# Output projection as seven half-size products in chunks, its input rows formed on GpSimd alone

## The reference

```python
h = rms_norm(x, in_norm_g)
q, k, v, g, xr, gr, m_ret, m_rnn = split(h @ w_in)
y_ret = (silu(g) * head_norm(retention(rot(q), rot(k), v))) @ w_ret_o
y_rnn = (rg_lru(conv(xr)) * gelu(gr)) @ w_rnn_o
mixed = sigmoid(m_ret) * y_ret + sigmoid(m_rnn) * y_rnn
x = x + mixed @ w_out                      # the output projection: 1024 x 1024 by 1024 x 1024
h = rms_norm(x, ffn_norm_g)
up = causal_depthwise_conv(h @ w_up)
x = x + (silu(gate) * val) @ w_down        # gate, val = the halves of up
out = rms_norm(x, final_norm_g)
```

## Time and profile before

| | |
|---|---|
| median of 3 runs | 1991.19 us (1989.85 to 1991.75) |
| span of the profiled execution | 1988.8 us |
| TensorE, VectorE, ScalarE, GpSimd busy | 99%, 71%, 47%, 17% of the span |
| `reto` | 28 chunks, 672 matmuls of 128x512 |
| output projection | 768 matmuls of 128x256, 1248.4 to 1345.7 us |

### The profile page before, as it was taken

The page is one execution under the profiler, slowest core; times in us unless marked ns, Lnnn a source line. Parts: engine busy times, 40 slices in busy tenths (PEclk is TensorE's granted clock), DMA queues, the critical chain, the costliest instruction groups (busy, mean ns, idle before and its releaser), DMA issues.

```text
span 1988.8 us, 24558 instructions
## 1 busy us (share of the span) xinstructions
PE 1961.3 (99%) x9208; PEld 1639.4 (82%) x9208; DVE 1418.8 (71%) x1621; ACT 934.4 (47%) x1182; POOL 333.9 (17%) x277
## 2 busy tenths in 40 slices
PE   8999999999999999999999999999999999999998
PEld 6888888888888888888888787997888888888887
DVE  7877876776755445667777658658987888776766
ACT  6443353343445555555555443346544544543335
POOL 2000010010392000067775003100000000000000
PEclk9999999999999999999999999999999999999999
DMA  6343554445697443465668555532222222256523
GB/s 259 117 169 137 180 181 157 169 158 179 206 327 281 159 159 127 148 200 173 206 190 256 199 196 194 184 112 84 85 91 78 84 84 84 74 191 234 199 96 132
DMA packets 222205, 325.07 MB, mean 163 GB/s; under 512 B 11824, under 2 KB 150448, under 8 KB 221872
## 3 DMA queue, kind: packets, MB, share of 16 engines
q1 hardware_dynamic: 196800, 232.84, 35.5%
q0 software_dynamic: 22608, 85.99, 11.0%
q10 hardware_dynamic: 2720, 5.24, 0.8%
HBM read 223.36 MB, written 100.66 MB: 163 GB/s over the span
## 4 chain that ended last, share of the span: by engine, by line
PE 83%; DVE 9%; ACT 3%; DMA 2%; issue 2%; POOL 1%; ACTq 0%; SPq 0%; DVEq 0%; POOLq 0%
PE ps L346 27%; PE ps L348 27%; PE ps L347 27%; DVE ws L329 1%; DMA stg<-scr_y 1%; DMA raw<-scr_q 1%; PE ps L1219 1%; POOL qkvs L949 1%; POOL state_s L955 1%; DVE ysr L2415 0%; DVE wx L2155 0%; POOL ws L968 0%; DVE wsr L2408 0%; ACT ri L1648 0%; DVE th L2337 0%
## 5 line engine op out<-in xcount | busy, mean ns | idle before, releaser
L1501 ACT ACTIVATE wx<-raw 128x1024 fp32r<-128x1024 f32 (+1 forms) x152 | 137.3, 905 | 252.3 <-DVE raw L2131 131.4
L346 PE MATMUL ps<-xs,wx 128*128 128x512 f32 x612 | 239.1, 391 | 2.1 <-DVE xs L2578 1.6
L348 PE MATMUL ps<-xs,wx 128*128 128x512 f32 x612 | 238.3, 389 | 0.0
L347 PE MATMUL ps<-xs,wx 128*128 128x512 f32 x612 | 238.2, 389 | 0.0
L2155 DVE TENSOR_TENSOR wx<-raw,wx 128x1024 fp32r<-128x1024 f32 (+1 forms) x152 | 158.9, 1047 | 30.4 <-ACT wx L1501 30.2
L346 PE MATMUL ps<-sc,wx 128*128 128x512 f32 x448 | 174.4, 389 | 0.0
L348 PE MATMUL ps<-sc,wx 128*128 128x512 f32 x448 | 174.3, 389 | 0.0
L347 PE MATMUL ps<-sc,wx 128*128 128x512 f32 x448 | 174.3, 389 | 0.0
L1536 ACT ACTIVATE ub<-ps 128x512 f32<-128x512 f32 x112 | 66.9, 597 | 159.1 <-PE ps L348 156.4
L346 PEld LDWEIGHTS ps<-xs,wx 128*128 128x128 f32 x612 | 114.9, 188 | 28.4 <-issue 2.7
L348 PEld LDWEIGHTS ps<-xs,wx 128*128 128x128 f32 x612 | 114.9, 188 | 24.1
(11 more groups left out here) (289 smaller groups left out, 4849.2 us busy)
## 6 DMA issues: line engine op xcount, KB each, us to landing
raw<-w_in SPq DMA_DIRECT2D x80, 512.0 KB, 5.5
scr<-ost POOLq DMA_DIRECT2D x32, 1024.0 KB, 5.2
raw<-w_up SPq DMA_DIRECT2D x44, 512.0 KB, 4.2
tq<-w_down SPq DMA_DIRECT2D x88, 128.0 KB, 2.7
scr_t<-tq POOLq DMA_DIRECT2D x22, 512.0 KB, 3.2
scr_h<-vt POOLq DMA_DIRECT2D x11, 1024.0 KB, 4.3
tr<-w_ret_o SPq DMA_DIRECT2D x64, 128.0 KB, 3.9
scr_q<-tr POOLq DMA_DIRECT2D x16, 512.0 KB, 5.2
```

Source lines behind the costliest of these rows:

```text
L346: pe.matmul(out, w(HI), x(HI), start=first, stop=False, skip_group_check=True)
L347: pe.matmul(out, w(HI), x(LO), start=False, stop=False, skip_group_check=True)
L348: return pe.matmul(out, w(LO), x(HI), start=False, stop=last, skip_group_check=True)
L1501: act.activation(dst, src, ACT.Copy).then_inc(sem["f_hi"], 1)
```

## The change

The output projection becomes seven products of 512x512 blocks (`O_W`), in 14 chunks, two per product, run as `reto`'s are: chunk numbers go on from 28, with the same buffers `wsr` and `ysr`. 24 matmuls of 128x512 per chunk, 336 in all.

- Four combined weight blocks (t1 to t4) are made on GpSimd during `reto`: eight pieces, `out_pieces` loads (SyncE, behind `reto_w` of chunks 6, 8, 10 and 12), `out_combine` computes and stores to `scr_o`.
- `mixed(n)` is on GpSimd alone, product and addition, into `mixm` (float32, four blocks); GpSimd also makes the four combined activation blocks, two additions of 128x1024 each (`mixed_sum`). Its order: 12 pieces, two sums, 4 pieces, six sums.
- ScalarE and VectorE split weights and activations chunk by chunk (`outp_w_hi`, `outp_y_hi`, `outp_w_lo`, `outp_y_lo`).
- VectorE adds partial products to `x1` (`out_add`, `out_add_row`); the order of the products (`O_W`, `O_BANK`) lets banks 4 to 7 accumulate b11, then t2, then t3, with reads between.
- The transposes of the first half of the tokens stand behind chunk 38 and inside chunk 39; the norms of the rows 4 to 7 stand behind the last additions.

The lines on which the rest turns:

```diff
+O_W = ["t4", "t1", "b11", "t2", "t3", "b22", "b21"]
+O_BANK = [4, 0, 4, 4, 4, 0, 4]
+O_FIRST = [True, True, True, False, False, False, True]
+O_LAST = [True, False, False, False, True, True, True]
...
             for i in range(4, R_CHUNKS):
                 reto_w(i)
+                if i >= 6 and i % 2 == 0 and (i - 6) // 2 < O_PIECES // 2:
+                    out_pieces(i - 6)
+                    out_pieces(i - 5)
...
+                if i in (24, 25, 26, 27):
+                    mix_more(i - 21)
+            for v in range(4):
+                sp_.wait_ge(sem[f"tr_out{v}"], 16 * (R_PIECES + O_PIECES) // 4)
+            out_w(R_CHUNKS)
             sp_.wait_ge(*late_count("ry_lo", R_CHUNKS - 4))
             sp_.dma_start(x1[:, 0:4, :], x_t[:, 0:4, :]).then_inc(sem["x_re"], 16)
...
+            out_w(R_CHUNKS + 1)
+            mix_more(7)
...
+            def out_combine(j):
...
+                pool.tensor_tensor(tr[:, v, 0:2, :], tr[:, v, 0:2, :], tr[:, v, 1:3, :], ALU.subtract).then_inc(late_sem("tr_st"), 1)
+                pool.wait_ge(*late_count("tr_st", done + 1))
+                pool.tensor_tensor(tr[:, v, 2, :], tr[:, v, 0, :], tr[:, v, 2, :], ALU.add).then_inc(late_sem("tr_st"), 1)
+                pool.wait_ge(*late_count("tr_st", done + 2))
+                pool.tensor_tensor(tr[:, v, 3, :], tr[:, v, 3, :], tr[:, v, 2, :], ALU.subtract).then_inc(late_sem("tr_st"), 1)
...
+            def mixed(n):
                 half, t = mix_at(n)
                 pool.wait_ge(sem[f"mx_in{n // 2 % 3}"], 32 * (n // 6 + 1))
                 pool.wait_ge(sem["acc"], mix_acc(n))
                 pool.tensor_tensor(msg[:, n % 6, :], msg[:, n % 6, :], yacc[:, t, half * HALF:(half + 1) * HALF],
                                    ALU.mult).then_inc(sem["mx_mul"], 1)
+                pool.wait_ge(sem["mx_mul"], n + 1)
+                pool.tensor_tensor(mixm[:, 2 * half + t // 4, t % 4, :], msg[:, n % 6, :], mrb[:, n % 6, :], ALU.add
+                                   ).then_inc(sem["mx_f"], 1)
...
+            for i in range(R_CHUNKS, R_CHUNKS + 11):
+                outp(i)
+            pe.wait_ge(sem["xn_done"], 8)
+            pe.wait_ge(sem["x1_done"], 12)
+            for k in range(4):
+                turn2(k, 0, 4 + k)
+            outp(R_CHUNKS + 11, (0, 1))
...
-            pe.wait_ge(sem["x1_done"], 16)
+            pe.wait_ge(sem["x1_done"], 18)
             for k, bank in ((0, 4), (1, 5), (2, 2), (3, 3), (4, 6), (5, 7)):
                 turn2(k, 1, bank)
...
+            def outp_w_lo(i):
+                u = i % 2
+                dve.wait_ge(*late_count("rw_hi", i + 1))
+                dve.tensor_tensor(wsr[u][:, LO, :, :], raw[:, 1, 2 * u * HALF:2 * (u + 1) * HALF].rearrange("p (k c) -> p k c", k=2),
+                                  wsr[u][:, HI, :, :].bitcast(F32), ALU.subtract).then_inc(late_sem("rw_lo"), 1)
...
+            for i in range(R_CHUNKS + 2, R_CHUNKS + 11):
+                outp_w_lo(i)
+                outp_y_lo(i)
+                p, c, _ = outp_at(i)
+                if c == 0 and p < 5:
+                    for t in (0, 2):
+                        out_add(p - 1, t, 2)
...
+            out_add(6, 2, 1)
             s_lo(A12, a12f, 0, 3)
             s_lo(A12, a12f, 1, 4)
-            out_add(6, 1)
-            prep_lo(0, 0, "b1")
+            out_add(6, 3, 1)
+            norm2(4)
+            norm2(5)
             combine_t4(0, 0)
             prep_lo(0, 0, "t4")
             prep_lo(0, 0, "t2")
...
+            norm2(6)
+            norm2(7)
```

More of the change, by code:

```diff
@@ L1277, in turn2 @@
                 last.then_inc(sem["tr_ps"], 1)
[L1279 to L1284, removed]
-                    pe.wait_ge(sem["acc"], 6)
[L1286 to L1303, removed]
-                if m == 5:
-                    for k in range(4, 8):
-                        pe.wait_ge(*late_count("a11_in", k - 3))
-                        turn2(k, 0, k)
@@ new lines, in outp_free, with outp @@
+            def outp_free(p, t):
+                if p == 0:
+                    pe.wait_ge(sem["acc"], 6)
+                elif p == 1:
+                    pe.wait_ge(sem["acc"], 7 + t)
+                elif p < 6:
+                    pe.wait_ge(sem["x1_done"], {2: 1, 3: 5, 4: 7, 5: 3}[p] + t // 2)
+                else:
+                    pe.wait_ge(sem["x1_done"], 12)
+                    pe.wait_ge(*late_count("a12_in", 4))
+            def outp(i, tiles=range(4)):
+                p, c, _ = outp_at(i)
+                u = i % 2
+                pe.wait_ge(*late_count("rw_lo", i + 1))
+                pe.wait_ge(*late_count("ry_lo", i + 1))
+                for t in tiles:
+                    if c == 0:
+                        outp_free(p, t)
+                    for k in range(2):
+                        last = mm3(pe, ps[:, O_BANK[p] + t, :], lambda q: ysr[u][:, q, k, t * P:(t + 1) * P],
+                                   lambda q: wsr[u][:, q, k, :], O_FIRST[p] and c == 0 and k == 0,
+                                   O_LAST[p] and c == 1 and k == 1)
+                    if c == 1:
+                        last.then_inc(sem["o_ps"], 1)
+                    elif t == 3:
+                        last.then_inc(late_sem("r_b"), 1)
@@ L1840, in _ @@
             act.wait_ge(fraw[0], 32)
-            act.wait_ge(blk[0], PAIR_FFN + 1)
+            act.wait_ge(*late_count("r_b", R_CHUNKS - 1 + 7))
             prep_hi(0, 0, "b1")
+            for t in range(4, 6):
+                norm2(t)
             act.wait_ge(sem["f_t4"], 1 + W_T)
@@ L1845, in _ @@
             prep_hi(0, 0, "t2")
-            for t in range(4, 8):
+            for t in range(6, 8):
                 norm2(t)
```

291 lines of the change are left out of this document (164 added, 127 removed).

## The result

| | before | after |
|---|---|---|
| median of the runs | 1990.52 us (4 runs, 1989.19 to 1991.75) | 1999.31 us (4 runs, 1997.51 to 1999.95) |
| ratio | | 1.0045, 95% interval 1.003 to 1.0059 |
| span of the profiled execution | 1988.8 us | 1995.9 us |

A forecast was written before the change was run, and what follows sets the result against it. The prediction took TensorE, busy 99% of the span, as the bound. Its terms (a) to (f) summed to +11.8 us on the profiled 1988.8, giving 2000.6, plus 2.4 for the median: 2003, range 1989 to 2014.

The forecast's parts named there:

- (a): Output projection matmuls on TensorE: 768 of 128x256 replaced by 336 of 128x512, -16.0 us.
- (b): `reto` chunks 6 to 12: GpSimd's combining of weight pieces delays VectorE's splits and sums, +8.3 us.
- (c): Tail of `reto` and border: 8.7 us of old losses removed, 4.1 of late splits remain, net -4.6.
- (d): Output projection's fourteen chunks: splits late beside GpSimd's sums and pieces, chunk 29's weights queued, one clock fall, +12.0 us.
- (e): First half's transposes: wait for late row additions and norms, +4.0 us and 1.7 of clock, +5.7.
- (f): Second half's transposes: wait for norms behind splits, +4.7 us and 1.7 of clock, +6.4.
- the turns: VectorE instructions with both inputs in SBUF and GpSimd's: the later waits until the other ends.
- The short end: VectorE splits against GpSimd's 128x1024 sums: lower bound of 1.1 us extra, not the whole 2.4; sum 3 us less.
- work wins: Rival: turns cost less because GpSimd slips into VectorE's rests; -7.6 us, 1983.6, chance 0.10.
- GpSimd as the bound: Rival: GpSimd's b11 pieces come late and TensorE waits; +8 to +10 on top, 2012, chance 0.22.
- The rival of no difference: Rival: (e) and (f) fall to 1 each, no clock falls, (b) 5; about -0 to +1, chance 0.05.

The follow-up runs named there:

- e12: Changed kernel with one piece of combined weights a chunk beside `reto` chunks 12 to 19, mixed-row loads moved to chunks 10, 19, 20; 1993.4 us, ratio 1.0012.
- e4: Changed kernel with the weights of chunks 28 and 29 issued ahead of the mixed-piece load and `x1` on SyncE's queue; 1996.1 us, ratio 1.0021.
- e6: Changed kernel with the first half's 32 transposes half a chunk later and chunk 40 waiting for each bank by itself; 1997.4 us, ratio 1.0033.
- e7: Changed kernel with the norms of rows 6 and 7 ahead of the t4 and t2 splits on ScalarE and VectorE; 1998.8 us, ratio 1.0033.
- e2: Changed kernel without GpSimd's 24 instructions that combine the weights, pieces still loaded and stored; 1996.2 us, ratio 1.0034.
- e5: Changed kernel with each of GpSimd's sums of 128x1024 cut in two of 128x512; 1997.3 us, ratio 1.0041.
- e10: Changed kernel with earlier weights, spread pieces, VectorE sums (later), later transposes, norms first, GpSimd resting until `reto` ends, second-FFN-block combinations behind norms; 1979.2 us, ratio 0.9943.

## Why the prediction was right

The sign, the place of each loss and the mechanism held. By its own steps, in us against the kernel before, by the ruler:

| step | predicted | measured | from |
|---|---|---|---|
| (a) matmuls | -16.0 | -16.0 | not contradicted: chunk pace 5.44 again |
| (b) pieces in `reto` | +8.3 | +6.3 | S1 133.5 against 127.2 without them there (e12) |
| (c) tail and border | -4.6 | -4.1 | S1 -1.8, S2 -0.6, clock behind the border -1.7 |
| (d) the stage's own waits | +12.0 | +8.5 | S3: 94.6 - 76.1 - 3.5 of transposes - (e) |
| (e) first transposes | +5.7 | +6.5 | gap 3.8, clock 2.7: 16 transposes take 3.3 us in place of 1.7, the next five matmuls 1.1 more |
| (f) second transposes | +6.4 | +6.2 | S4 |
| sum | +11.8 | +7.4 | S1 to S4: +7.7 |

**(b)** mis-sized by 2.0. Three chunks lose 1.6, 1.2 and 1.8 us, 4.6 in all, as the turns have it; I had 2.5 for each, because I put a GpSimd instruction between any two of VectorE's. 1.7 more come from weights that land late, which I had at nothing. There is a slip in my working besides: four turns of 0.94 are 3.8, not 3.4, so by its own rule the term was about 9.5, and the slip brought it nearer by luck.

In both engines' rows the later instruction waited for nearly the whole of the other: 3.42 is 1.14 and 2.28 of waiting, beside a sum of 2.41, and halves bring it to 2.31. The short end, 1.1 of extra, is refuted. That is the rule of the Trainium skill (SBUF — State Buffer, the section on the two separate sides), by which the loser waits for the whole instruction, and the trace agrees.

**(d)** mis-sized by 3.5, most of it in the sums: 2.8, 2.4 and 0.5 predicted, gaps of 1.2 and 2.3 measured. GpSimd's schedule was close (first twelve pieces done 4.9 us later than said, last sum at 1294.0 against 1290). But I let both splits wait a whole sum in two chunks, and in only one did they (3.07 and 3.41); in the other chunks the weight split slipped through at 1.21 to 1.23. Pieces alone cost some 0.3 in each of two chunks (5.74 and 5.73 us long), where I had 0.7. Chunk 29's 3.2 and 1.7 came as 2.4 and 1.7, by the cause named: the queue.

**(c)** right in size by luck, half wrong in cause. I reckoned the remaining loss of 4.1 with VectorE's turns alone. By the starts of matmuls the changed kernel still loses 1.9 in the tail's six chunks (before 4.2) and 2.8 at the border (before 3.4 and 1.7 of clock), and the border was weights: e4 has them issued 13.3 us before the last `reto` matmul, the changed kernel 9.0. Read this way (b) is 6.8 and (c) -4.6, with the same sum: e12, from which the table takes (b), has a late chunk of its own at the end of `reto`. I had named the queues that the loads are moved past, yet not that SyncE waits in order for GpSimd's pieces.

**(e)** and **(f)** right in mechanism, (f) in size too: rows added late, norms behind the splits, and a clock that falls behind the gap; behind the first gap it stayed at half for longer than in the earlier trace rows (0.50 over 4 us, 0.80 over the next 4), which makes (e) 0.8 larger than I had it. e6 and e7 bear them out by moving the gap, and show that each has a second instruction close behind the one that I named.

So the forecast lay 4 us too high by the ruler, 3 by the medians: (b) and (d) too large by 5.5, (e) too small by 0.8. The rivals: work wins was out, the turns hold. GpSimd as the bound was out too: no split waited for L1066. (The rival of no difference was summed wrongly: its own terms give about -3, not 0.) What could not be settled: how much of e2's gain (6.7 by the ruler, 3.1 by the medians) a typical execution sees. The runs' spread leaves room for both.

## What to carry to other kernels

Work given to GpSimd "because it is idle" costs VectorE up to one whole GpSimd instruction for each of its own that reads SBUF twice: put it where VectorE has rests (e12, 6 us), in short instructions (e5, by its trace), or where VectorE reads PSUM, and reckon it by the longest single instruction, not by busy shares. That is an upper bound: here some 60% of it came (4.6 of 7.5 us in `reto`, 3.5 of 5.7 beside the sums), since not every instruction meets another. A faster stage needs its inputs at a faster pace: before each large load and each in-order wait on the queue ask which weights stand behind it (e4). The new algorithm was worth it once its side work was placed: -0.65% in place of +0.45%, with the same matmuls.

## What the runs showed of the hardware

- Even an instruction of almost no work, with one input, can wait its turn. It is 8 elements a partition; in the kernel before, with GpSimd at rest, it takes 0.17 us, in e10 it ends with GpSimd's addition at about 1252.6, and in e4 it meets a sum of 128x1024 (in this order):

```profile
1266.51 0.17 DVE L2558 TENSOR_SCALAR neg_g<-prm 128x8 f32<-128x8 f32 x1
1251.46 1.14 DVE L2653 TENSOR_SCALAR neg_g<-prm 128x8 f32<-128x8 f32 x1
1257.29 2.36 DVE L2667 TENSOR_SCALAR neg_g<-prm 128x8 f32<-128x8 f32 x1
```

- The turn is mutual. GpSimd's additions of 128x256, 0.73 us at the least and 0.76 in the median, took 1.60 beside VectorE:

```profile
1115.17 1.60 POOL L1047 TENSOR_TENSOR tr<-tr 128x256 f32<-128x256 f32 x1
1116.85 1.60 POOL L1049 TENSOR_TENSOR tr<-tr 128x256 f32<-128x256 f32 x1
```

- The clock does not fall after every gap of one length. Behind the same gap of 2.3 us beside the last sums, changed kernel and then e7_norms_first (windows, clock third from the end):

```profile
1294.00:1298.00 4.00, 4.00 (x19) 3.30 (x19) 2.31 (x3) 0.00 (x0) 0.03 (x1) 1.00 0.40 125
```
```profile
1300.00:1304.00 4.00, 4.00 (x12) 3.14 (x11) 2.22 (x2) 0.00 (x0) 0.00 (x0) 0.57 0.44 122
```

That is 1.7 us, and a gap may or may not bring it. From 1100 to 1400 us the clock is at half for 3.4 us in all in the kernel before, for 13.7 in the changed one, for 20.5 in e12 and never in e10. It fits the spread between executions of one kernel: of e7's eight runs the fastest (1994.0 us) has a mean granted clock of 0.998, the slowest three (2002.2 to 2002.9) 0.994 to 0.995. So count a gap at its length and a chance of the clock.
